# Token halves pass the border between phases one by one in a transformer stack on one core

## What is computed

```python
def rms_norm(x, g):
    return x * lax.rsqrt(jnp.mean(x * x, axis=-1, keepdims=True) + EPS) * g
def swiglu(h, w13, w2):
    a, g = jnp.split(h @ w13, 2, axis=-1)
    return (jax.nn.silu(a) * g) @ w2
# first stack
x = x + 0.5 * swiglu(rms_norm(x, ffn1_norm[l]), ffn1_w13[l], ffn1_w2[l])
...
# second stack
x = x + 0.5 * rms_norm_2(swiglu_2(rms_norm_2(x, g[0]), ffn_w_in[i, 0], ffn_w_out[i, 0]), g[1])
x = x + rms_norm_2(mixer(rms_norm_2(x, g[2])), g[3])
x = x + 0.5 * rms_norm_2(swiglu_2(rms_norm_2(x, g[4]), ffn_w_in[i, 1], ffn_w_out[i, 1]), g[5])
```

## Time and profile before

| what | us |
| --- | --- |
| median of 3 runs (lowest, highest) | 3773.41 (3771.87, 3777.15) |
| the profiled execution's own time | 3778.8 |
| its span | 3777.0 |
| PE busy | 3436.2 (91%) |
| DVE busy | 2186.5 (58%) |
| ACT busy | 1803.9 (48%) |
| POOL busy | 92.5 (2%) |

### The profile page before, as it was taken

The page is one execution under the profiler, slowest core; times in us unless marked ns, Lnnn a source line. Parts: engine busy times, 40 slices in busy tenths (PEclk is TensorE's granted clock), DMA queues, the critical chain, the costliest instruction groups (busy, mean ns, idle before and its releaser), DMA issues.

```text
span 3777.0 us, 49507 instructions
## 1 busy us (share of the span) xinstructions
PE 3436.2 (91%) x18184; PEld 2940.8 (78%) x18184; DVE 2186.5 (58%) x2330; ACT 1803.9 (48%) x2261; POOL 92.5 (2%) x208
## 2 busy tenths in 40 slices
PE   7987899999779899998899998789999989998799
PEld 6876677878677788787787877678787978787687
DVE  5565465555655555556555565555656655556555
ACT  4454444444554454445444453344445544444444
POOL 0000000000000000000000000100000000000000
PEclk9987899999878999998999996679999999999899
DMA  6653345545433455454354543235454444454254
GB/s 236 218 188 112 109 169 181 181 178 189 145 106 120 153 189 189 176 180 148 142 179 177 189 167 123 72 106 189 178 191 178 161 150 178 176 191 168 100 200 167
DMA packets 105050, 618.45 MB, mean 164 GB/s; under 512 B 10816, under 2 KB 19008, under 8 KB 34656
## 3 DMA queue, kind: packets, MB, share of 16 engines
q1 hardware_dynamic: 84288, 562.07, 41.4%
q10 hardware_dynamic: 20640, 54.71, 4.3%
HBM read 615.62 MB, written 9.50 MB: 166 GB/s over the span
## 4 chain that ended last, share of the span: by engine, by line
PE 83%; DVE 7%; ACT 4%; issue 3%; DVEq 1%; POOL 1%; DMA 0%; ACTq 0%; POOLq 0%
PE ps L1520 32%; PE ps L1524 16%; PE ps L1584 6%; PE ps L1583 6%; PE ps L1585 6%; PE ps L1541 2%; PE ps L1542 2%; PE ps L1543 2%; PE ps L1559 2%; PE ps L1683 1%; PE ps L1672 1%; DVE wlo L985 1%; ACT v L633 1%; PE ps L1697 1%; PE ps L1698 1%
## 5 line engine op out<-in xcount | busy, mean ns | idle before, releaser
L1520 PE MATMUL ps<-xhl,whi 128*128 128x512 f32 x4944 | 1734.7, 401 | 34.8 <-DVEq L401 34.8
L985 DVE TENSOR_TENSOR wlo<-raw,whi 128x2048 fp32r<-128x2048 f32 x526 | 1204.1, 2292 | 784.4 <-ACT whi L597 784.3
L1524 PE MATMUL ps<-xhl,wlo 128*128 128x256 f32 x4944 | 1289.6, 281 | 0.0
L597 ACT CAST whi<-raw 128x2048 fp32r<-128x2048 f32 x526 | 999.8, 1904 | 226.5 <-PE ps L1585 128.0
L1520 PEld LDWEIGHTS ps<-xhl,whi 128*128 128x128 f32 x4944 | 905.4, 190 | 217.2 <-issue 41.8
L1524 PEld LDWEIGHTS ps<-xhl,wlo 128*128 128x128 f32 x4944 | 946.6, 191 | 55.4
L1584 PE MATMUL ps<-wlo,ht 128*128 128x512 f32 x1056 | 417.2, 395 | 0.0
L1583 PE MATMUL ps<-whi,ht 128*128 128x512 f32 x1056 | 417.1, 395 | 0.0
L1585 PE MATMUL ps<-whi,ht 128*128 128x512 f32 x1056 | 416.6, 395 | 0.0
L670 ACT COPY tg<-ps 128x512 f32<-128x512 f32 x132 | 77.5, 587 | 430.9 <-PE ps L1520 430.9
L1585 PEld LDWEIGHTS ps<-whi,ht 128*128 128x128 f32 x1056 | 198.3, 188 | 48.1
(11 more groups left out here) (242 smaller groups left out, 3718.1 us busy)
## 6 DMA issues: line engine op xcount, KB each, us to landing
raw<-stream SPq DMA_DIRECT2D x528, 1024.0 KB, 4.8
bias<-rel_bias ACTq DMA_DIRECT2D x80, 256.0 KB, 2.7
gain<-gains ACTq DMA_DIRECT2D x19, 1024.0 KB, 4.7
bias<-fixed_bias ACTq DMA_DIRECT2D x40, 256.0 KB, 2.6
rel_bias<-rel_vectors SPq DMA_DIRECT2D x16, 512.0 KB
x<-x_tokens ACTq DMA_DIRECT2D x1, 1024.0 KB, 4.8
y_tokens<-x ACTq DMA_DIRECT2D x1, 1024.0 KB, 3.9
cst<-constants ACTq DMA_DIRECT2D x1, 670.0 KB, 6.6
```

The source lines that it names most:

```text
L597: nc.scalar.copy(whi[:, slot, :], raw[:, slot, :]).then_inc(sem["hi_ready"], 1)
L985: nc.vector.tensor_tensor(wlo[:, slot, :], raw[:, slot, :], whi[:, slot, :].bitcast(F32), ALU.subtract).then_inc(sem["lo_ready"], 1)
L1520: wide = lambda: pe.matmul(ps[:, bank, 0:2 * half], hi[:, k, col0:col0 + P], src[:, k0 + k, :], start=first and k == 0, stop=last and k == ...
L1524: e = pe.matmul(ps[:, bank, 0:half], lo[:, k, col0:col0 + P], src[:, k0 + k, 0:half], start=False, stop=False)
```

## The change

The two token halves pass a border separately. On each engine the order becomes: half 0 through all stages, with half 1 behind it, and the splits of the next phase's steps 1 and 2 among them. PE no longer takes part in `between`: the transposes move into the next phase (`arrive`), and PE waits for a half's low parts alone (`arrived`, new semaphore `x_low`). The last two `down` steps, and the last two steps of `wout`, go by halves: both steps for half 0, then both for half 1. The first pair of an FFN is made by token columns (`token_cols`, 256 columns a product, banks 4 and 5), half 0 first; the transposes of half 1 stand after three quarters of half 0's products. Its silu(a) * g is therefore by token and is turned by four transposes in bank 6. A projection after a border starts with a two-step v group by halves (`lead_of`); in the diff, nsa and moba phases the v groups are moved ahead of q and k, and the stream is packed in the new order. gqa2 still begins with kv: there both halves are awaited. POOL goes by halves as well.

```diff
-        project(f("q", 0, 2), f("k", 0, 2), t("v", 0, 512, 4, 2, 1))
+        project(t("v", 0, 512, 4, 2, 1), f("q", 0, 2), f("k", 0, 2))
...
-            project(f("q", 0, 4), f("cmp", 0, 2))
+            project([Group("v", None, 2, KD, 2 * P, 0)], f("q", 0, 4), f("cmp", 0, 2))
...
-            project(f("k", 0, 1), t("v", 0, 256, 8, 1, 1), f("k", 4, 1), t("v", 256, 256, 8, 1, 1),
-                    t("gate", 0, 48, 8, 1, 1))
+            project(f("k", 0, 1), f("k", 4, 1), t("gate", 0, 48, 8, 1, 1))
...
-            by_four = [g for n in range(4) for g in f("q", 4 * n, 1) + f("k", 4 * n, 1) + t("v", 256 * n, 256, 8, 1, 1)]
+            by_four = [g for n in range(4) for g in t("v", 256 * n, 256, 8, 1, 1) + f("q", 4 * n, 1) + f("k", 4 * n, 1)]
...
+                step = after_of(ph).step
+                first_statistics(0)
+                if per_token == 2:
+                    last_statistics(0)
+                    first_statistics(1)
+                if ph.gains == 0:
+                    split(0)
+                split(step + 1)
+                high_parts(0)
+                if per_token == 2:
+                    last_statistics(1)
+                else:
+                    first_statistics(1)
+                split(step + 2)
+                high_parts(1)
...
+                def first_pair(tt):
+                    if tt == 0:
+                        act.wait_ge(sem["ag_made"], base(ph, "ag_made") + 1)
+                    else:
+                        multiplied(ph.step + 1)
+                    nc.scalar.activation(silu[:, tt, :], ps[:, 4 + tt, 0:T], ACT.Silu).then_inc(sem["silu_first"], 1)
+                first_pair(0)
                 split(ph.step + 3)
-                multiplied(ph.step + 1)
-                half_g(0)
+                first_pair(1)
+                act.wait_ge(sem["tposed"], base(ph, "tposed") + 1)
+                nc.scalar.copy(ht[:, 0, :, 0, :], ps[:, 6, :].rearrange("p (k t) -> p k t", k=2))\
+                    .then_inc(sem["hi_made"], 1)
...
+                if ph.after == "post":
+                    gained(0)
+                added(0)
+                if ph.final:
+                    final_norm(0)
+                normed(0)
+                if ph.after == "post":
+                    gained(1)
+                else:
+                    added(1)
                 if ph.gains == 0:
                     split(0)
+                low_parts_of(0)
+                if ph.after == "post":
+                    added(1)
+                if ph.final:
+                    final_norm(1)
+                split(step + 1)
+                normed(1)
+                low_parts_of(1)
+                split(step + 2)
...
+            def arrive(ph, tt):
+                last = before_of(ph)
+                pe.wait_ge(sem["xn_ready"], base(last, "xn_ready") + tt + 1)
+                for half in range(2):
+                    n, k0 = 2 * tt + half, 4 * half
                     for k in range(4):
                         e = pe.transpose(ps[:, n, k * P:(k + 1) * P], o[:, tt, (k0 + k) * P:(k0 + k + 1) * P], ident)
                     e.then_inc(sem["tposed"], 1)
+            def arrived(ph, tt):
+                last = before_of(ph)
+                pe.wait_ge(sem["x_low"], base(last, "x_low") + 2 * tt + 2)
...
+                def first_pair(tt, turn_between):
+                    for part in range(2):
+                        use(ph.step + part)
+                        w = step_parts(ph.step + part, KD, 2 * P)
+                        dst = ps[:, 4 + tt, part * T:(part + 1) * T]
+                        token_cols(dst, w, 0, 2 * P, xhl, tt, range(KD // 2))
+                        if turn_between and part == 1:
+                            arrive(ph, 1)
+                        e = token_cols(dst, w, 0, 2 * P, xhl, tt, range(KD // 2, KD))
+                        if tt == 1:
+                            e.then_inc(sem["step_used"], 1)
+                    if tt == 0:
+                        e.then_inc(sem["ag_made"], 1)
+                arrive(ph, 0)
+                arrived(ph, 0)
+                first_pair(0, True)
+                arrived(ph, 1)
+                first_pair(1, False)
+                use(ph.step + 2)
+                w = step_parts(ph.step + 2, KD, 2 * P)
+                feature_tile(0, w, 0, xhl)
+                for tt in range(TT):
+                    pe.wait_ge(sem["h_first"], base(ph, "h_first") + tt + 1)
+                    for kk in range(2):
+                        e = pe.transpose(ps[:, 6, kk * T + tt * P:kk * T + (tt + 1) * P],
+                                         h[:, tt, kk * P:(kk + 1) * P], ident)
+                e.then_inc(sem["tposed"], 1)
+                feature_tile(1, w, P, xhl).then_inc(sem["step_used"], 1)
+                pe.wait_ge(sem["ht_first"], base(ph, "ht_first") + 1)
+                down(ph.step + 3, first=True)
+                up(ph.step + 4, 2)
...
+                for tt in range(TT):
+                    for i in range(2):
+                        c = end - 2 + i
+                        if tt == 0:
+                            pe.wait_ge(sem["ht_ready"], base(ph, "ht_ready") + last - 1 + i)
+                            use(c)
+                        w = step_parts(c, 2, D)
+                        for kk in range(2):
+                            e = rows_by(w, i, tt, kk, False, i == 1)
+                        if tt == 1:
+                            e.then_inc(sem["step_used"], 1)
+                    if tt == 0:
+                        e.then_inc(sem["acc_half"], 1)
...
+                arrive(ph, 0)
+                if ph.groups[0].dest == "v":
+                    arrived(ph, 0)
+                    product(0, 0)
+                    arrive(ph, 1)
+                    arrived(ph, 1)
+                    product(0, 1)
+                else:
+                    arrive(ph, 1)
+                    arrived(ph, 0)
+                    arrived(ph, 1)
+                    product(0, 0)
+                    product(0, 1)
...
-                for i in range(4):
+                for i, tt in ((0, 0), (0, 1), (1, 0), (1, 1), (2, 0), (3, 0), (2, 1), (3, 1)):
```

More of the change, by code:

```diff
@@ L390, in wait, with before_of, after_of, rounds_of @@
             eng.wait_ge(semaphore, value)
+        def before_of(ph):
+            n = phases.index(ph)
+            return phases[n - 1] if n else None
+        def after_of(ph):
+            return phases[phases.index(ph) + 1]
+        def rounds_of(ph):
+            return ([ph.factor] if ph.after == "post" else []) + [1.0] * (ph.final + ph.pre)
+        def follows_between(ph):
+            return before_of(ph).kind == "between"
         def enter(eng, me, ph):
+            last = before_of(ph)
+            overlapped = me == "pe" and last is not None and last.kind == "between"
+            before = last.before if overlapped else ph.before
             for e in ("pe", "act", "dve", "pool"):
@@ L558, in between @@
             def between(ph):
[L560 to L563, removed]
+                rounds = rounds_of(ph)
+                for tt in range(TT):
+                    for r, factor in enumerate(rounds):
+                        n = len(rounds) * tt + r
                         ms = stat[:, n:n + 1]
@@ L1568, in up, with rows_by @@
                     feature_tile(bank + 1, w, P, xhl).then_inc(sem["step_used"], 1)
-                def down(c, pair, j=None, first=False, last=False):
-                    pe.wait_ge(sem["ht_ready"], pair + (base(ph, "ht_ready") + 1))
+                def rows_by(w, buffer, tt, kk, first, last):
+                    hh, hl = (ht[:, buffer, kk, part, tt * P:(tt + 1) * P] for part in (0, 1))
+                    for half in range(2):
+                        cols = slice(512 * half, 512 * half + 512)
+                        dst = acc[:, 2 * tt + half, :]
+                        pe.matmul(dst, hh, w[0][:, kk, cols], start=first and kk == 0, stop=False)
+                        pe.matmul(dst, hh, w[1][:, kk, cols], start=False, stop=False)
+                        e = pe.matmul(dst, hl, w[0][:, kk, cols], start=False, stop=last and kk == 1)
+                    return e
@@ L2030, in stream_of @@
             for n in range(4):
-                for part in range(3):
+                for part in (2, 0, 1):
                     columns(m, part * D + 2 * P * n, 1)
```

289 lines of the change are left out of this document (154 added, 135 removed).

## The result

| what | us |
| --- | --- |
| before, median of 6 runs beside the changed kernel (lowest, highest) | 3772.64 (3771.5, 3778.97) |
| after, median of 6 runs (lowest, highest) | 3790.34 (3786.11, 3795.1) |
| ratio, 95% interval | 1.0046 [1.0034, 1.0059] |
| profiled execution after, its span | 3787.1, 3785.3 |

The forecast was 3778.5. The measured time lies 11.8 us above it: inside the whole range (3761 to 3797), but outside the forecast's own case (3771 to 3786) and nearer to the 3794 of rival 2, the slower one with the clock.

The account below looks back on a forecast made before the run. TensorE carried 83% of the chain that ended last, so its standing and clock set the time. Border gains of -37.8 and other terms of +42.4 net +4.6, taking the median from 3773.4 to 3778.5 us; range 3761 to 3797.

Parts of the forecast that it names:

- the forecast's own case: Whole kernel: the summed forecast holds, 3771 to 3786 us; chance 0.45.
- rival 2: Clock falls at plain borders (five: +8.5) and behind moba's four waits (about 1.7 each): +15, 3794 us; chance 0.24.
- Post borders: Borders normed first, after an FFN or wout: next phase's first product 5.1 us after PE's last; four save 16.2 us.
- Plain borders: Borders where sums are added plainly: next products 2.8 us after PE's last, clock stays up; three before FFNs save 15.6.
- The FFN's end: Last down steps by halves: PE waits 1.2 us for the last pair's ht; twelve FFNs, +14.4 us.
- The FFN's start: First pair made by tokens, so h needs four transposes, 0.5 us each FFN; +6.0 us for twelve.
- gqa2: Two borders where kv needs both halves: first product 14.2 us after PE's last, against 11.1; +8.5 us for both.
- Moba: Order v, q, k uncovers k's copies before four scores: new waits less old ones and border gain, +15 us.
- Rival 1: Moba's weave absorbs its new waits: moba costs +2, total 3765.5 us; chance 0.25.
- Rival 3: The halves don't overlap: half 1 so late that all 17 borders end 1.5 us later, 3804 us; chance 0.06.
- borders after a weave: Three borders (1827, 3057, 3571): two steps complete 22.8 us after PE's last product, against 23.3; -1.4 us for three.
- 1509: The border that norms twice: first product 8.8 us after PE's last, two steps complete at 23.8 against 26.2, -2.4 us.

Follow-up runs that it names:

- the first execution: The changed kernel as it is, the first of its three profiled executions: span 3785.3 us.
- all parts together: Changed kernel with new moba and diff group orders, other gqa2 queue order, and a mixed FFN-end order before plain borders: 3761.36 us, ratio 0.9973.

## Why the prediction was right or wrong

- **Post borders, right.** S was forecast at E+5.1 and is E+4.8 to 5.7. From E to the first product on ht the four borders gained 3.5, 4.7, 1.9 and 3.6 us (29.57, 30.74, 28.01 and 29.75 before), 13.7 in all; the forecast's 16.2, less 0.5 each for the FFN's start, is 14.2. The rows of DVE and POOL above show their links of the chain as they were counted, with POOL's 0.8.
- **Plain borders, right, and with them the first half of rival 2 wrong.** S = E+3.0 at four and E+3.4 at the first (2.8 forecast), E to first product on ht 26.5 to 21.9 (-4.6; -4.7 forecast). The clock stayed up at thirteen of fifteen; where it fell in front of an FFN, that FFN began its products on ht 1.5 us later (23.4). The forecast let the clock stay up on the word of one row, and the time came out by it; whether for the row's reason, that transposes hold the clock, is not shown, since a border of only 3.0 us would explain it as well. In the mixer behind E = 213.6 this gain was not seen, as forecast: the attention starts at E+48.5 (48.1 forecast, 48.8 before), after a stand of 10.04 us.
- **The FFN's end, right.** 1.02 us by twelve, 12.3 for 14.4. **The FFN's start** (+6.0) has no run of its own; it is in the sums above.
- **gqa2, right within 1.2.** S = E+14.4 and 14.6 for the forecast 14.2, and 17 us at half clock at the border for 7 and 10 before, for which the forecast had taken 1 to 1.5 each.
- **Moba, right in the standing, short by the clock.** +15.2 us of standing for +15, partly by luck (misses of 2.7, 2.4 and 0.5 in its terms cancel); the 0 to 4.8 us of lower clock behind the four waits were put at nothing. Rival 1 is refuted: all four waits for k stand at 5.3 us or more, and only 6.1 us of the weave's own waits went.
- **Rival 3 didn't come**: half 1's turns follow PE's work without a stand at the post borders into an FFN and into nsa; at moba's they wait 0.83 us.
- **Where the 10 us were missed** is the sum of what was set to nothing. From E to the first product on ht the borders after a weave were given 0.0 each; measured are 0.0 to +0.4, +1.2 to +1.7 and -0.1. 1509 was given -1.9 and has -1.1. Mixers were given -1.0 and have +0.8. With gqa2's 1.2 and moba's 3.1 the misses make 10 us, nearly all on one side. In most of these places, in the first execution, PE is at half clock for as long as before or longer: after a weave 10.2 us each (before 10.2, 6.8, 10.2), at gqa2 17 each (7 and 10), in moba 31 to 44 (24). Rival 2 had named the clock, priced at +15 and put half of it in the wrong place.

## What to carry to other kernels

Before moving a producer to the end of a phase, look at what ran beside its epilogue: here k's copies (5.2 us on ACT and DVE) lay under v's products, and an order chosen for one border took the cover away four times, which cost 12 to 16 us of standing. Such a reorder is best tested alone and in both directions, since here one part held nearly the whole loss. For a kernel whose executions differ by several us in stretches that no edit touches, compare stretches over several executions, not spans of one.

## What the runs showed that was not expected

- One and the same kernel has, in the same stretch with the same instructions, 82 to 99 us at half clock before and 79 to 96 after, and the stretch takes 348 or 355 us. The kernel before repeats its second stack within 0.1 us each stretch in three executions; the changed kernel does not: moba 166.3 to 171.9, first gqa2 122.6 to 125.1, nsa 285.3 to 288.3.
- How long PE stood doesn't by itself say whether the clock falls. Stands of 0.36 and 1.56 us around eight transposes left it up in most executions, and so did 1.36 and 1.56 (all parts together, two borders). With a first stand of 2.39 it fell 2.3 us after E, and with one of 2.60 (before, E = 570.5) only 4.4 us after E.
- POOL's `tensor_scalar` on 128 x 1 numbers took 0.19 us in 33 of 62 cases in the changed kernel, all without a DVE operation beside it or with one that reads PSUM. Beside a weight split it took 0.98 us, or 1.84 to 1.95 (at the start and all five plain borders), and beside a norm 0.72 to 1.27.
